# Latent pages turned by block transfers and VectorE, with six weight units on chip in place of eight

## The reference

```
q_lat  = einsum('bqhd,chd->bqhc', q_nope, w_uk)
s_past = einsum('bqhc,bkc->bhqk', q_lat, lat_past) + einsum('bqhr,bkr->bhqk', q_rope, kr_past)
s      = concat([s_past * MLA_SCALE, where(incl, s_new * MLA_SCALE, -inf)])
p      = softmax(s)
ctx    = einsum('bhqk,bkc->bqhc', p[..., :past], lat_past) + (the new token's part)
```

## Time and profile before

| | |
|---|---|
| median of 3 runs | 1265.94 us (1265.73 to 1266.15) |
| the profiled execution, its own time | 1266.02 us |
| its span, first to last instruction | 1264.2 us |
| busy: TensorE, its weight loads | 1250.9, 1022.8 us |
| busy: VectorE, ScalarE, GpSimd | 549.7, 250.5, 153.0 us |
| mean granted TensorE clock | 0.998 of full |
| moved by DMA | 198.49 MB, 157 GB/s in the mean |

### The profile page before, as it was taken

The page is one execution under the profiler, slowest core; times in us unless marked ns, Lnnn a source line. Parts: engine busy times, 40 slices in busy tenths (PEclk is TensorE's granted clock), DMA queues, the critical chain, the costliest instruction groups (busy, mean ns, idle before and its releaser), DMA issues.

```text
span 1264.2 us, 18049 instructions
## 1 busy us (share of the span) xinstructions
PE 1250.9 (99%) x7142; PEld 1022.8 (81%) x7142; DVE 549.7 (43%) x1387; ACT 250.5 (20%) x640; POOL 153.0 (12%) x210
## 2 busy tenths in 40 slices
PE   8999999999999999999999999999999999999997
PEld 6878777776888888888888787777778888888886
DVE  7866646323235333321178746463241453324212
ACT  3432414311100111110033324243111011111000
POOL 2012442010000000020001134511000000000000
PEclk9999999999999999999999999999999999999999
DMA  9433576357454444464454344755564544444440
GB/s 342 155 100 101 134 254 227 130 188 170 122 152 148 147 143 147 148 225 150 148 154 142 100 115 150 249 205 177 140 173 126 149 143 149 150 150 150 151 138 35
DMA packets 93971, 198.49 MB, mean 157 GB/s; under 512 B 41680, under 2 KB 42736, under 8 KB 91072
## 3 DMA queue, kind: packets, MB, share of 16 engines
q1 hardware_dynamic: 84624, 156.15, 40.4%
q0 software_dynamic: 8768, 40.84, 9.4%
q10 hardware_dynamic: 496, 0.36, 0.1%
HBM read 183.86 MB, written 9.25 MB: 153 GB/s over the span
## 4 chain that ended last, share of the span: by engine, by line
PE 95%; DVE 4%; ACT 1%; issue 0%; DMA 0%; SPq 0%; DVEq 0%; ACTq 0%
PE banks L573 77%; PE banks L1063 2%; PE banks L1076 1%; PE banks L1111 1%; PE banks L1074 1%; PE banks L968 1%; PE banks L717 1%; DVE arena L1715 1%; PE banks L996 1%; PE banks L675 0%; PE banks L1012 0%; DMA arena<-in_x 0%; DVE arena L2114 0%; PE banks L873 0%; PE banks L590 0%
## 5 line engine op out<-in xcount | busy, mean ns | idle before, releaser
L573 PE MATMUL banks<-arena 128*128 128x264 f32 x4512 | 1032.3, 388 | 5.7 <-DVE arena L1609 4.9
L573 PEld LDWEIGHTS banks<-arena 128*128 128x128 f32 x4512 | 851.0, 190 | 169.2 <-issue 13.2
L1217 ACT ACTIVATE arena<-banks 128x256 f32<-128x256 f32 (+8 forms) x252 | 92.6, 391 | 403.7 <-PE banks L573 293.2
L2217 DVE TENSOR_SCALAR arena<-arena 128x256 f32<-128x256 f32 x44 | 18.2, 414 | 130.2 <-ACT arena L1217 130.0
L2250 DVE SCALAR_TENSOR_TENSOR arena<-banks,arena 128x264 f32<-128x264 f32 x16 | 6.9, 433 | 134.2 <-PE banks L573 134.2
L2431 POOL COPY arena<-arena 128x2 f32<-128x2 f32 x44 | 13.7, 310 | 377.6 <-ACT arena L1217 275.9
L1248 ACT ACTIVATE arena<-banks 128x264 f32<-128x264 f32 x32 | 12.6, 392 | 130.6 <-PE banks L573 130.6
L2110 DVE COPY arena<-banks 128x512 f32<-128x512 f32 x24 | 16.6, 690 | 36.7 <-PE banks L1063 36.5
L1529 ACT ACTIVATE arena<-arena 128x256 f32<-128x256 f32 x44 | 18.4, 417 | 66.3 <-DVE arena L2219 66.3
L2224 DVE SCALAR_TENSOR_TENSOR arena<-arena 128x256 f32<-128x256 f32 x44 | 18.7, 426 | 26.6 <-ACT arena L1529 26.6
L2229 DVE TENSOR_TENSOR arena<-arena,banks 128x256 f32<-128x256 f32 x42 | 17.7, 422 | 26.4 <-PE banks L573 26.3
(11 more groups left out here) (447 smaller groups left out, 1072.5 us busy)
## 6 DMA issues: line engine op xcount, KB each, us to landing
arena<-in_weights SPq DMA_DIRECT2D x229, 512.0 KB, 3.6
arena<-in_weights SPq DMA_DIRECT2D x113, 256.0 KB, 3.5
arena<-in_s POOLq DMA_DIRECT2D x2, 2048.0 KB, 10.9
out_ss_o<-arena POOLq DMA_DIRECT2D x16, 256.0 KB, 3.1
arena<-in_mla_w POOLq DMA_DIRECT2D x4, 1024.0 KB, 6.7
arena<-arena SPq DMA_DIRECT2D x64, 64.0 KB, 2.4
arena<-in_c POOLq DMA_DIRECT2D x4, 512.0 KB, 6.3
out_sc_o<-arena POOLq DMA_DIRECT2D x16, 128.0 KB, 3.8
```

The source lines that it names most:

```text
L573: mm = nc.tensor.matmul(dst, ring[:, at_:at_ + 128], rhs[:, j, :], start=(start and j == 0), stop=(stop and j == k - 1))
L1217: return A(dst, src, ACT.Copy, scale=scale)
L2217: link(ts(cv, fc[:, j % 3, 0:TP], w[0], par[:, Q_FB + j:Q_FB + j + 1], ALU.mult, ALU.add))
```

## The change

- `SLOTS` is 6; SyncE is up to 5 units ahead. The 2048 columns that come free are `spare_blocks`.
- All eight pages are laid out in blocks by SyncE's transfers and turned by VectorE. TensorE's transposes and the copies out of their banks go, on TensorE, ScalarE and VectorE.
- The blocks of pages 2 and 3 lie in `spare_blocks` in turn, those of pages 6 and 7 in `lat[0]` and `lat[1]` as before, and those of pages 0, 1, 4 and 5 in `ltt[:, n % 2]` itself, where they are turned in place.
- So the transfers of a page wait: pages 0 to 2 for `uq` 7 (and the gathered page), page 3 for the turns of page 2, page 4 for the scores of page 2, page 5 for those of page 3, pages 6 and 7 for `cx` 0.
- `mark()` writes down in front of which weight unit the transfers of a page stand in SyncE's program. With the counts of the schedule these are units 43 (page 0), 44 (1), 45 (2), 51 (3), 53 (4), 56 (5), 57 (6) and 58 (7). As unit u waits for the start of unit u-5, page 3 waits for unit 46 (the half in front of page 2's scores), page 5 for unit 51 (the first half behind context 0).
- On TensorE, 3 halves are moved from between pages and later products to in front of page 3: `pages(3)` comes after `half(3)`.
- VectorE's turns are spread in its own order (`turn(n, parts)`): pages 0 and 1 in halves around `divided(1)`, page 4 before `newest(0)`, page 5 after `combined(0)`, page 6 with `wc` 0 before it and `wc` 1 behind it, page 7 after `wc` 2.
- GpSimd's gathers of pages 5 to 7 wait for the scores of page n-5 in place of the transposes of page n-4.

```diff
-SLOTS = 8
+SLOTS = 6
@@ schedule()
+    def mark(*sequences):
+        at_ = (34 + piece[0]) // 2 + SLOTS - 1
+        for n in sequences:
+            while at_ in marks:
+                at_ += 1
+            marks[at_] = n
...
+    mark(0, 1)
     add("uq", 8, "V"); add("bcK", 4, "V")
     add("uk", 4); add("uv", 2); add("ql")
-    add("sc", 4, "V"); half(2); add("sc", 4, "V", 4); half(8)
+    add("sc", 4, "V"); half(2); add("sc", 4, "V", 4); mark(2); half(8)
...
     for n in range(4):
+        if n == 2:
+            mark(3)
+        if n == 3:
+            half(3)
         pages(n)
-    add("ss"); half(1); ...; add("lsum", 1, "V"); add("cx")
-    at_context = (34 + piece[0]) // 2
+    mark(4)
+    add("ss"); half(1); ...; add("lsum", 1, "V"); mark(5); add("cx")
+    mark(6, 7)
@@ SyncE
+        def blocks(n):
+            return spare_blocks if n in (2, 3) else lat[n - 6] if n >= 6 else ltt[:, n % 2].rearrange("p i n -> p (i n)")
...
             def blocks_of_latents(l, n):
-                sp.wait_ge(*out(l, "cx", 0))
+                if n < 3:
+                    sp.wait_ge(*out(l, "uq", 7))
+                elif n == 3:
+                    sp.wait_ge(*at(l, "lat_turned", 12))
+                elif n == 5:
+                    sp.wait_ge(*out(l, "ss", 0))
+                elif n == 4:
+                    sp.wait_ge(*at(l, "page_scored", 3))
+                else:
+                    sp.wait_ge(*out(l, "cx", 0))
...
-                if u % UNITS in (BLOCKS_AT, BLOCKS_AT + 1):
-                    blocks_of_latents(u // UNITS, 6 + u % UNITS - BLOCKS_AT)
+                if u % UNITS in BLOCKS_AT:
+                    blocks_of_latents(u // UNITS, BLOCKS_AT[u % UNITS])
@@ TensorE, pages(n)
-                    if n < 6:
-                        for i in range(4):
-                            b = claim("ltr", 4 * n + i)
-                            for q in range(4):
-                                r_ = 4 * i + q
-                                mm = nc.tensor.transpose(b[:, q * P:(q + 1) * P], lat[n][:, r_ * P:(r_ + 1) * P], ident)
-                            mm.then_inc(out_ready, 1)
                     half(1)
-                    if n < 6:
-                        pe.wait_ge(*evac(l, "ltr", 4 * n + 2))
-                        pe.wait_ge(*evac(l, "ltr", 4 * n + 3))
-                        pe.wait_ge(*at(l, "key_turned", n + 1))
-                    else:
-                        pe.wait_ge(*at(l, "lat_turned", 4 * (n - 5)))
+                    pe.wait_ge(*at(l, "lat_turned", 4 * (n + 1)))
...
-                for n in range(4):
+                for n in range(3):
                     pages(n)
+                half(3)
+                pages(3)
@@ ScalarE
-                for n in range(4):
-                    pages(n)
-                half(2)
+                half(9)
                 powers(0)
...
@@ VectorE
+                def turn(n, parts):
+                    if parts[0] == 0:
+                        dve.wait_ge(*at(l, f"lat_in{n}", 32))
+                        if n >= 2:
+                            dve.wait_ge(*scored(n - 2))
+                        V.transpose(krt[:, n % 2, :], key[n]).then_inc(*up("key_turned"))
+                        dve.wait_ge(*at(l, f"lat_blocks{n}", 256))
+                    for i in parts:
+                        V.transpose(ltt[:, n % 2, i, :], blocks(n)[:, 512 * i:512 * i + 512]).then_inc(*up("lat_turned"))
...
                 divided(0)
-                half(4)
+                turn(0, (0, 1))
+                half(1)
+                turn(0, (2, 3))
+                half(3)
                 divided(1)
-                half(5)
+                turn(1, (0, 1))
+                half(2)
+                turn(1, (2, 3))
+                half(3)
...
-                for n in range(4):
-                    pages(n)
+                half(2)
+                turn(2, (0, 1, 2, 3))
+                half(4)
+                turn(3, (0, 1, 2, 3))
+                half(1)
                 top(0, 1)
                 half(3)
                 total(0)
+                turn(4, (0, 1, 2, 3))
                 newest(0)
                 half(2)
                 combined(0)
-                pages(4)
-                half(2)
-                pages(5)
-                half(4)
-                pages(6)
-                pages(7)
+                turn(5, (0, 1, 2, 3))
+                half(1)
+                half(2)
+                turn(6, (0, 1, 2, 3))
+                half(5)
+                turn(7, (0, 1, 2, 3))
+                half(2)
                 top(1, 2)
@@ GpSimd
                 for n in range(5, NB):
-                    pool.wait_ge(*out(l, "ltr", 4 * (n - 4) + 3))
+                    pool.wait_ge(*at(l, "page_scored", n - 4))
```

More of the change, by code:

```diff
@@ L143, in pages @@
     def pages(n):
-        if n < 6:
-            s.extend(("ltr", 4 * n + i, "AV"[i % 2]) for i in range(4))
         half(1)
     for n in range(4):
+        if n == 2:
+            mark(3)
+        if n == 3:
+            half(3)
         pages(n)
-    add("ss"); half(1); add("mxT", 1, "V"); half(1); add("mxB", 1, "V"); half(3); add("lsum", 1, "V"); add("cx")
-    at_context = (34 + piece[0]) // 2
+    mark(4)
+    add("ss"); half(1); add("mxT", 1, "V"); half(1); add("mxB", 1, "V"); half(3); add("lsum", 1, "V"); mark(5); add("cx")
+    mark(6, 7)
     half(2); add("cmb", 1, "V")
@@ L160, in schedule @@
     add("fd", 8, "V")
-    return s, at_context + SLOTS - 1
+    return s, marks
 SCHED, BLOCKS_AT = schedule()
@@ L201 @@
     decay_masked=1, diag_set=3, ffn_conv=22, ffn_sconv=2, ffn_stanh=2, ffn_tail=22, ffn_tanh=22, ffn_zeros=1, fh_loaded=16,
-    hidden=2, hidden_norm=16, norm_raw=16, norm_square=16, norm_sum=14, hist_loaded=16, key_copied=2, key_turned=8, lat_turned=8, **{f"lat_blocks{n}": 256 for n in (6, 7)}, **{f"lat_in{n}": 32 for n in range(8)},
+    hidden=2, hidden_norm=16, norm_raw=16, norm_square=16, norm_sum=14, hist_loaded=16, key_copied=2, key_turned=8, lat_turned=32, **{f"lat_blocks{n}": 256 for n in range(8)}, **{f"lat_in{n}": 32 for n in range(8)},
     inverse=1, inverse_turned=1, m_loaded=64, mdecay_exp=1, mdecay_in=4, mdecay_masked=1, merged=8, mla_q=16, mla_kv=16,
@@ L245, in build @@
         ring = fix.take(SLOTS * 1024)
+        spare_blocks = fix.take(2048)
         const = fix.take(N_CONST)
@@ L458, in build @@
         last_rms = bank("fd", 1)[:, 0:TT]
+        def blocks(n):
+            return spare_blocks if n in (2, 3) else lat[n - 6] if n >= 6 else ltt[:, n % 2].rearrange("p i n -> p (i n)")
         def quarter_of_latents(n, b, q):
-            return (lat[n - 6][32 * q:32 * q + 32, 512 * b:512 * b + 512].rearrange("i (r j) -> i r j", r=NR),
+            return (blocks(n)[32 * q:32 * q + 32, 512 * b:512 * b + 512].rearrange("i (r j) -> i r j", r=NR),
                     lat[n][32 * b:32 * b + 32, :].rearrange("i (r q j) -> i r q j", r=NR, q=4)[:, :, q, :])
@@ L1057, in pages @@
                         sb = bank("ss", g)
[L1058 to L1071 removed]
+                    half(1)
+                    pe.wait_ge(*at(l, "lat_turned", 4 * (n + 1)))
                     for i in range(4):
[L1073 to L1074 removed]
+                        nc.tensor.matmul(sb[32 * i:32 * i + 32, :], ql_pad[:, g, s_, :], ltt[:, n % 2, i, :],
                                          start=(s_ == 0), stop=False, skip_group_check=True)
@@ L1459, in _ @@
                 values(1)
[L1461 to L1477, removed]
                 def powers(g):
@@ L1499, in _ @@
                 context(0)
-                half(2)
-                pages(4)
-                half(2)
-                pages(5)
-                half(6)
+                half(12)
                 half(3)
@@ L2050, in _, with scored @@
                 last.then_inc(*up("query_blocks"))
+                def scored(n):
+                    if n % 4 == 3:
+                        return out(l, "ss", n // 4)
+                    return at(l, "page_scored", 3 * (n // 4) + n % 4 + 1)
+                def turn(n, parts):
[7 more added lines that the diff above has]
+                        V.transpose(ltt[:, n % 2, i, :], blocks(n)[:, 512 * i:512 * i + 512]).then_inc(*up("lat_turned"))
                 def masked(g):
@@ L2091, in _ @@
                 V.tensor_copy(ckb, heads(bank("ckB")[0:32, 0:2 * P], P)).then_inc(*read("ckB"))
[L2092 to L2115, removed]
                 def top(g, n):
```

11 lines of the change are left out of this document (5 added, 6 removed).

## The result

The changed kernel takes **1320.03 us** (median of 4 runs, 1318.66 to 1320.90) against 1266.05 us before (4 runs, 1265.73 to 1266.74): 1.0425 times as long, 95% interval 1.0407 to 1.0443. It was forecast slower at 1287.1, in a range of 1268 to 1301: the side was right, the size was 21 us in place of 54. The profiled execution took 1318.66 us, its span is 1316.9 us, 52.7 more than before.

A forecast was written before the change was run, and what follows sets the result against it. TensorE, busy 99% of the span, was taken to bound the kernel, with SyncE's issues setting new waits. 1266.0 - 21.1 (transposes) + 37.8 (waits) + 4.4 (clock) = 1287.1 us, range 1268 to 1301.

The forecast's parts named there:

- What goes, 21.1 us: On TensorE, the page transposes of both layers go, saving 21.1 us by start-to-start time, 10.6 us a layer.
- A page costs SyncE 11.3 us: In SyncE's queue, a page's 16 block transfers take 11.3 us to issue, 12.5 with a weight unit.
- Pages 0 to 2 hidden but for 0.5 us: Early in each layer, these transfers hide; turns of pages 0 and 1 delay wa 0 and wa 3, costing 0.5 us.
- The bound of 3.2 with no cover: Cost of the late wa 0 and wa 3 if the two banks covered none of it: 3.2 us.
- Page 3, 5.6 us: Before page 3's scores, TensorE waits 5.6 us a layer, as its blocks must await page 2's turn and unit 46.
- Pages 5 to 7, 2.4 + 3.9 + 6.5 = 12.8 us: TensorE waits a layer: 2.4 us for page 5, 3.9 for wc 1's evacuation behind page 6's turn, 6.5 for page 7.
- The waits in all, 18.9 a layer: All new TensorE waits: 0.5+5.6+2.4+3.9+6.5 = 18.9 us a layer, 37.8 in both.
- The ring, 0: Weight stream: six units in place of eight lead by 18.3 us instead of 25.6; no cost taken.
- the bounds of 0 and 4: Limits given for the smaller weight ring's cost: 0 and 4 us a layer, if several units come late.
- The clock, 4.4 us: TensorE falls to half clock behind half of the four waits of 5.6 and 6.5 us, 2.2 us each: 4.4 us.

The follow-up runs named there:

- experiment 7: Kernel before, ring of eight, with only pages 0 and 1 added to the pages by block transfers, gathers 5 to 7 as in the changed kernel: 1259.57 us.
- experiment 2: Changed kernel with GpSimd's gathers of pages 5 to 7 held back until page 3 is turned: 1313.97 us.
- experiment 1: Kernel before with a ring of six weight units in place of eight: 1266.17 us, ratio 1.0002.
- experiment 3: Changed kernel with each 64 KB block transfer as 32 rows of 2 KB in place of 512 runs of 128 bytes, scores wrong: 1294.25 us.
- experiment 6: Changed kernel with eight of each page's sixteen block transfers issued by GpSimd in place of SyncE: 1305.00 us.
- experiment 8: As experiment 7, with page 4 by block transfers too and pages 6 and 7 issued half by SyncE, half by GpSimd: 1258.43 us.

## Why the prediction was wrong

By its own steps, for layer 0, in the order in which it made them:

- *What goes, 21.1 us.* Right. The transposes are gone from the chain, and experiment 7 won 6.4 of 7.1 us with two of the six pages.
- *A page costs SyncE 11.3 us.* **This is the first step that failed,** and the waits went wrong with it. It was taken from two pages that had no gathers beside them (10.84 and 11.55 us, 11.2 in the mean; the 0.1 above it matters little), and I put it on all eight. Six of the eight do take 10.7 to 11.8. Page 0 takes 18.3 and page 3 20.3; experiment 2 shows for page 3 that the nine extra are the gathers' doing. For page 0 the same is argued, from its long issues between 207.1 and 218.4 and the two gathers at 204.9 and 207.4 that land 8.5 us later, and no run moved these gathers away. The change to GpSimd's waits stood in the diff, and I gave it no place in the sum.
- *Pages 0 to 2 hidden but for 0.5 us.* Too low by 3.4: with page 0 seven microseconds late, page 1 was too (its turn began at 234.0), wa 3 waited behind its turn and cost TensorE 3.1 us, and unit 45's weights 0.8. The bound of 3.2 with no cover came nearer, but by luck: it was worked out with page 0 in time.
- *Page 3, 5.6 us.* 13.9, of which 5.0 are left with the gathers away.
- *Pages 5 to 7, 2.4 + 3.9 + 6.5 = 12.8 us.* 3.0 + 3.1 + 4.8 = 10.9. Mechanism, places and order as predicted; pages 6 and 7 took SyncE 10.7 and 11.3 us.
- *The waits in all, 18.9 a layer.* 28.7 and 26.3: 55.0 us for 37.8, 17.2 too few.
- *The ring, 0.* 0.8 us a layer, the wait for unit 45 that is counted above, and within the bounds of 0 and 4; experiment 1 shows 0 for the ring alone.
- *The clock, 4.4 us.* Right in kind, and the second term that was much too small: 17.2. From start to start, the work behind wa 3's wait took 1.7 us more than at full clock (235.66 to 240.72, 5.06 us; before, the same products run from 231.86 to 235.21), behind page 3's 3.0 (from 282.01 to 288.74 in 6.73 us, which took 3.76 before), behind page 6's 1.5 and behind page 7's 2.2: 8.4 us. In layer 1 it is 1.7 behind wa 3's wait, 2.9 behind page 3's, 1.7 behind page 5's, 0.1 behind page 6's and 2.4 behind page 7's: 8.8. I took a fall in half of the waits of pages 3 and 7 alone, at 2.2 each; it came in all four of these, and behind shorter ones, of 3.1 us and in layer 1 of 2.2.

The Trainium skill ("TensorE: Matmul & The Clock Gate", section "HAM oscillation — how this bites in real kernels") says that gaps which wait for data put TensorE back on the half clock each time. The trace agrees for the waits for pages 3 and 7, of 4.8 to 13.9 us: the granted clock is 0.50 just behind each. For shorter waits the length does not decide it: behind 2.2 us in layer 1 the clock was 0.59, behind page 5's 3.0 us in layer 0 it stayed at 1.00.

The sum with what was measured: -21.1 + 54.7 (55.0 less the 0.3 that TensorE waited there before) + 17.2 = 50.8 us. The span grew by 52.7. 0.4 of the rest are lost before the end of uq (201.32 for 200.96), where the waits for the norm's tiles are longer at the start; 1.5 us I can't place. Of the 33 us between the forecast and the result, the waits are 17.2 and the clock 12.8.

The rule on SyncE's queue in the Trainium skill ("DMA: Bandwidth & Descriptors", section "Issuing engines are not separate DMA queues"), by which an issue's time is usually small next to its transfer, does not hold for these: 0.63 us to issue beside the 0.38 us of DMA work that I estimated, and by experiment 3 that is hardly a matter of the runs. Its other sentence, that DMAs of all issuers interleave on the same engines, is what I should have weighed against the gathers. The trace agrees that other issuers' DMAs are felt: page 3's issues took 20.3 us beside gathers and 11.5 without (experiment 2).

## What to carry to other kernels

When the trace gives a price for a transfer, note what else was on the DMA engines at that time, and ask it again for each place to which the transfer is moved: here 11 us was 20 beside gathers, and in an in-order queue all that stands behind pays too. Move to another engine only as many pieces as have their own gap: two pages of six gained 6.4 us, all six lost 54. Where TensorE bounds at full clock, a new wait costs its length and a part again for the clock behind it: here 17 us on 55.

## What the runs showed of the hardware that was not expected

- A transfer of 64 KB from SBUF to SBUF takes SyncE 0.63 us to issue as 512 runs of 128 bytes and 0.59 as 32 rows of 2 KB; a weight load (256 or 512 KB) takes 0.33 us in the median.
- Beside gathers of 1.25 MB each, a single issue of short runs lasted up to 6.7 us, and two or three gathers added 7 to 11 us to a page's issues. With long rows the issues went on at their pace, and the landing took up to 8.1 us.
- GpSimd's block transfers slowed SyncE's, and not the other way round: GpSimd issued at 0.65 us each, and SyncE's issues beside it took 1.2 and 1.3 us in the median in place of 0.63 (experiments 6 and 8), with no gathers in flight. What of this lies in the queues and what in the DMA engines was not tested.
- The granted clock fell to 1.2 GHz behind waits of 2.2, 3.1 and 13.9 us in a stream that was otherwise dense, but not behind one of 3.0 us, and matmuls of 128x264 lasted 647 ns at it, as in the earlier trace rows.
